# Hybrid encoder layer on one core: h of four blocks and two thirds of the adaLN modulation moved from the front phase into the projection phase

## What is computed

```python
ada = jax.nn.silu(c) @ p['w_ada'][l] + p['b_ada'][l]
sh1, sc1, gt1, sh2, sc2, gt2 = jnp.split(ada[:, None, :], 6, axis=-1)
h = rms_norm(x, p['norm_pre_mix'][l]) * (1 + sc1) + sh1
x = x + gt1 * rms_norm(token_mixer(h, p, l), p['norm_post_mix'][l])
h = rms_norm(x, p['norm_pre_ffn'][l]) * (1 + sc2) + sh2
y = expert_choice_ffn(h, p['w_router'][l], p['w_gate_e'][l], p['w_up_e'][l], p['w_down_e'][l])
return x + gt2 * rms_norm(y, p['norm_post_ffn'][l])
```

## Time and profile before

| | us |
|---|---|
| median of three runs | 3905.72 |
| range of the runs | 3895.16 to 3907.7 |
| the profiled execution | 3897.49 |
| its span | 3895.8 |
| front phase | 0 to 168.9 |
| projections and attention | 168.9 to about 972 |
| gated linear attention | about 972 to 1679 |
| mix | 1679 to about 2250 |
| route, experts, final | to 3895.8 |

### The profile page before, as it was taken

One profiled execution on the slowest core, in us unless ns is written; L12 is line 12 of the kernel. 1 busy time (PEld: TensorE's weight loads), 2 busy tenths in 40 slices (PEclk: granted clock), 3 DMA queues, 4 the chain that ended last, 5 costly groups with the idle time before them and its releaser, 6 DMA issues. The chain is left out here.

```text
span 3895.8 us, 56808 instructions
## 1 busy us (share of the span) xinstructions
PE 3536.0 (91%) x21432; PEld 2934.1 (75%) x21432; DVE 2169.3 (56%) x3920; ACT 1593.3 (41%) x2374; POOL 651.0 (17%) x709
## 2 busy tenths in 40 slices
PE   7699999998889999979999928999999999999991
PEld 3377777766667777757878728999999999999991
DVE  1344534554568888745545465565555555555555
ACT  1344545544334344334444303444444444443442
POOL 0010100101023443402322200011110001000005
PEclk9799999999999999989999858999999999999996
DMA  9733432421754554456555434555555555555567
GB/s 303 238 120 87 136 115 86 130 86 64 232 169 137 168 155 138 120 168 204 187 185 187 154 135 157 157 167 169 170 174 161 165 164 175 172 162 166 162 218 272
DMA packets 544843, 634.46 MB, mean 163 GB/s; under 512 B 77560, under 2 KB 431896, under 8 KB 543776
## 3 DMA queue, kind: packets, MB, share of 16 engines
q1 hardware_dynamic: 506960, 493.72, 40.4%
q0 software_dynamic: 35840, 123.75, 10.0%
q10 hardware_dynamic: 1872, 14.68, 0.9%
HBM read 505.20 MB, written 126.88 MB: 162 GB/s over the span
## 5 line engine op out<-in xcount | busy, mean ns | idle before, releaser
L2414 DVE TENSOR_TENSOR moe_w_lo<-moe_w_raw,moe_w_hi 128x2048 fp32r<-128x2048 f32 x192 | 439.9, 2291 | 371.5 <-ACT moe_w_hi L2362 338.5
L103 PE MATMUL moe_pg<-moe_x_hi,moe_w_hi 128*128 128x320 f32 x2048 | 635.5, 310 | 1.4 <-DVE moe_x_lo L2452 1.4
L104 PE MATMUL moe_pg<-moe_x_lo,moe_w_hi 128*128 128x320 f32 x2048 | 633.8, 309 | 0.0
L105 PE MATMUL moe_pg<-moe_x_hi,moe_w_lo 128*128 128x320 f32 x2048 | 633.8, 309 | 0.0
L2362 ACT CAST moe_w_hi<-moe_w_raw 128x2048 fp32r<-128x2048 f32 x192 | 364.9, 1900 | 158.2 <-DMA moe_w_raw<-in_w_gate_e_dram 81.2
L103 PEld LDWEIGHTS moe_pg<-moe_x_hi,moe_w_hi 128*128 128x128 f32 x2048 | 385.3, 188 | 2.4 <-issue 1.5
L104 PEld LDWEIGHTS moe_pg<-moe_x_lo,moe_w_hi 128*128 128x128 f32 x2048 | 385.4, 188 | 0.6
L105 PEld LDWEIGHTS moe_pg<-moe_x_hi,moe_w_lo 128*128 128x128 f32 x2048 | 385.3, 188 | 0.0
L103 PE MATMUL gla_pd<-gla_h_hi,gla_w_hi 128*128 128x512 f32 x640 | 261.1, 408 | 34.5 <-DVE gla_h_lo L1012 31.9
L103 PE MATMUL pa_pu<-pa_h_hi,pa_w_hi 128*128 128x512 f32 (+1 forms) x560 | 226.9, 405 | 37.4 <-DVE pa_h_lo L644 37.4
L105 PE MATMUL gla_pd<-gla_h_hi,gla_w_lo 128*128 128x512 f32 x640 | 252.4, 394 | 0.0
(11 more groups left out here) (326 smaller groups left out, 7664.0 us busy)
## 6 DMA issues: line engine op xcount, KB each, us to landing
moe_w_raw<-in_w_gate_e_dram SPq DMA_DIRECT2D x64, 1024.0 KB
moe_w_raw<-in_w_up_e_dram SPq DMA_DIRECT2D x64, 1024.0 KB
moe_w_raw<-in_w_down_e_dram SPq DMA_DIRECT2D x64, 1024.0 KB
gla_w_raw<-in_w_in_dram SPq DMA_DIRECT2D x80, 512.0 KB, 4.0
pa_w_raw<-in_w_in_dram SPq DMA_DIRECT2D x35, 1024.0 KB
front_w<-in_w_ada_dram SPq DMA_DIRECT2D x24, 1024.0 KB, 11.9
scratch_gate<-gla_sg POOLq DMA_DIRECT2D x80, 256.0 KB, 2.3
mix_sg<-scratch_gate SPq DMA_DIRECT2D x40, 512.0 KB, 4.6
```

What stands on the lines that cost most here:

```text
L103: pe.matmul(out, w_hi, x_hi, start=start, stop=False)
L104: pe.matmul(out, w_hi, x_lo, start=False, stop=False)
L105: return pe.matmul(out, w_lo, x_hi, start=False, stop=stop)
L2414: dve.tensor_tensor(w_lo[:, m % 2], w_raw[:, m % 2], w_hi[:, m % 2].bitcast(F32), ALU.subtract).then_inc(s_wlo, 1)
```

## The change

It edits three phases.

In the front, only the first eight chunks of `w_ada` and block 0 remain. All eight chunks have buffers of their own. cS is widened to 32 columns, the products of the eight k go to four groups of 32 PSUM partitions (two each), the four partial sums are added by a product with `pick`, which also turns them. The 2 MB of h are stored in two halves by SP. The gates and the second modulation are gone from here.

In the projections, each of the 16 tiles of blocks 1 to 4 is made in the block before: `load_x` on SP, `squares` on ACT, `rms` on POOL, `norm_x` on DVE, `turn_x` on TensorE (eight transposes into two of the three banks, behind units `TURNS`), `first_half` on ACT and `second_half` on DVE (behind units `EVICTS`), `store_h` on POOL. `load_h` moves from chunk 7 to chunk 9 and waits for the stores. In the last block, 16 units of `ada_rows` use the remaining 16 chunks of `w_ada`, loaded by POOL, and their rows go to scratch `ada`. Unit v is computed like k, and a new unit `vt` turns it with four transposes. The low-rank unit stacks the high and low half of its weights into 64 columns (16 products for 24), and `la` is one fp32r product of 96 rows that hold high, low and high halves.

In the mix phase, block 0 reads the rows of `ada` and makes `K.a2`, `K.b2`, `K.gate1` and `gate2` from them between its first units; the router bias moves by up to two chunks. `K.gate1` is now allocated behind the gated linear attention.

```diff
-    K.gate1 = K.sb("gate1", [P, 2, D])
+    K.cS = K.sb("cS", [P, KD, 2])
...
+                for n in range(NCH):
+                    sp.dma_start(w[:, n], wv[:, :, n * CW:(n + 1) * CW]).then_inc(s_w[n], 16)
+                    if n == 1:
+                        sp.dma_start(x[:], block_of(I, 0)).then_inc(s_x, 16)
+                for i in range(2):
+                    sp.wait_ge(s_ha, 2 * i + 2)
+                    sp.wait_ge(s_hd, 2 * i + 2)
+                    sp.dma_start(S["hT"][0][:, 4 * i * BLK:4 * (i + 1) * BLK],
+                                 hT[:, 4 * i:4 * i + 4].rearrange("p k n -> p (k n)")).then_inc(s_st, 16)
+                sp.wait_ge(s_st, 32)
...
+                    pe.wait_ge(s_w[n], 16)
                     for k in range(KD):
-                        mm = pe.matmul(pa[m % 2][0:2, n % 2 * CW:n % 2 * CW + CW], cS[:, k, :], w[:, n % RAW, k, :],
-                                       start=k == 0, stop=k == KD - 1)
+                        mm = pe.matmul(pa[n // 2][k % 4 * 32:k % 4 * 32 + 32, n % 2 * CW:n % 2 * CW + CW], cS[:, k, :],
+                                       w[:, n, k, :], start=k < 4, stop=k >= 4)
                     mm.then_inc(s_chunk, 1)
 
...
+                for n in range(NCH - 2):
+                    chunk(n)
                 pe.wait_ge(s_id, 4)
...
+BLOCK_UNITS = [("k", 0, 0), ("v", 0, 0), ("q", 0, 1), ("vt", 0, None), ("q", 1, 1), ("q", 2, 2), ("q", 3, 2), ("l", 0, 3),
...
+TURNS = {4: 0, 7: 1, 12: 2, 16: 3}
+SQUARES = {1: 0, 5: 1, 8: 2, 11: 3}
+NORMS = {2: 0, 6: 1, 10: 2, 14: 3}
+EVICTS = {5: 0, 8: 1, 13: 2, 17: 3}
+N_ADA = 16
+ADA = {j: n for n, j in enumerate([j for j, u in enumerate(BLOCK_UNITS) if u[0] not in ("la", "vt")][:N_ADA])}
+
...
+                    if b:
+                        for n in range(2):
+                            sp.wait_ge(s_hst[n], 32 * b)
...
+                    if b < NB - 1:
+                        load_x(4 * b)
+                        load_x(4 * b + 1)
...
+                        if c in (7, 8) and b < NB - 1:
+                            load_x(4 * b + c - 5)
+                        if c == 9 and b < NB - 1:
...
+                        wait(act, s_lat, b)
+                        act.copy(vT, bank[:]).then_inc(s_evac, 1)
+                    elif kind == "vt":
...
+                        act.copy(rank[0], bank[2 * RANK:4 * RANK, :]).then_inc(s_g, 1)
+                        act.wait_ge(s_gs, b + 1)
+                        act.copy(gl[0:2 * RANK, :], rank[1])
+                        act.copy(gl[4 * RANK:6 * RANK, :], rank[1]).then_inc(s_ghi, 1)
...
+                def squares(i):
+                    act.wait_ge(s_x[i % 2], 16 * (i // 2 + 1))
+                    wait(act, s_rstd, i)
+                    for n in range(2):
+                        wait(act, s_sq, 2 * i + n)
+                        act.activation(junk, x[:, i % 2, n * D // 2:(n + 1) * D // 2], ACT.Square,
+                                       accum_out=ss[:, n:n + 1]).then_inc(s_sq, 1)
+
+                def first_half(i):
+
+                    n = UNIT_NO["turn", i, 0]
+                    act.wait_ge(s_unit, n + 2)
+                    for k in range(KD // 2):
+                        ins = act.activation(x[:, i % 2, k * P:(k + 1) * P], pu[n % BANKS][:, k * P:(k + 1) * P], ACT.Identity,
+                                             bias=K.b1[:, 1, k:k + 1], scale=K.a1[:, 1, k:k + 1])
+                    ins.then_inc(s_ha, 1)
+
+                def read_ada(i):
+                    n = UNIT_NO["ada", i, 0]
+                    act.wait_ge(s_unit, n + 1)
+                    wait(act, s_rst[i % 2], 64 * (i // 2))
+                    act.copy(row[:, i % 2], pu[n % BANKS][:, 0:CW]).then_inc(s_row, 1)
+
                 split_w(0)
                 split_h(0)
...
+                        if b < NB - 1 and j in EVICTS:
+                            first_half(b * TPB + EVICTS[j])
+                        if b < NB - 1 and j in SQUARES:
+                            squares(b * TPB + SQUARES[j])
+                        if b == NB - 1 and j in ADA:
+                            read_ada(ADA[j])
...
+                def second_half(i):
+
+                    n = UNIT_NO["turn", i, 1]
+                    dve.wait_ge(s_unit, n + 1)
+                    for k in range(KD // 2, KD):
+                        ins = dve.tensor_scalar(x[:, i % 2, k * P:(k + 1) * P], pu[n % BANKS][:, (k - 4) * P:(k - 3) * P],
+                                                K.a1[:, 1, k:k + 1], K.b1[:, 1, k:k + 1], ALU.mult, ALU.add)
+                    ins.then_inc(s_hd, 1)
...
+                            dve.wait_ge(s_g, b + 1)
+                            dve.tensor_tensor(rank[1], pu[n % BANKS][0:2 * RANK, :], rank[0], ALU.add).then_inc(s_gs, 1)
+                            dve.wait_ge(s_ghi, b + 1)
+                            dve.tensor_tensor(gl[2 * RANK:4 * RANK, :], rank[1], gl[0:2 * RANK, :].bitcast(F32),
+                                              ALU.subtract).then_inc(s_glo, 1)
...
+                def store_h(i):
+                    pool.wait_ge(s_ha, i + 1)
+                    pool.wait_ge(s_hd, i + 1)
+                    b, t = i // TPB + 1, i % TPB
+                    pool.dma_start(S["hT"][b].rearrange("p (k n) -> p k n", n=BLK)[:, :, t * P:(t + 1) * P],
+                                   x[:, i % 2].rearrange("p (k n) -> p k n", n=P)).then_inc(s_hst[i % 2], 16)
+
+                ada = I["w_ada"][0].rearrange("(k p) n -> p k n", p=P)[:, :, 2 * D:6 * D]
+
+                def load_ada(i):
+                    if i >= N_ADA:
+                        return
+                    if i == 0:
+                        for n in range(2):
+                            pool.wait_ge(s_hst[n], 32 * (NB - 1))
+                    else:
+                        pool.wait_ge(s_unit, UNIT_NO["ada", i - 1, 0] + 1)
+                    for n in range(2):
+                        pool.dma_start(x[:, n].rearrange("p (k n) -> p k n", n=CW),
+                                       ada[:, 4 * n:4 * n + 4, i * CW:(i + 1) * CW]).then_inc(s_ada[n], 16)
+
...
+                    what, b, j = ORDER[n - BANKS]
+                    if what == "turn":
+                        pe.wait_ge(s_hd if j else s_ha, b + 1)
+                        return
+                    if what == "ada":
+                        pe.wait_ge(s_row, b + 1)
+                        return
...
+                def turn_x(i, half):
+                    n = UNIT_NO["turn", i, half]
+                    bank_free(n)
+                    pe.wait_ge(s_xn, i + 1)
+                    for k in range(4 * half, 4 * half + 4):
+                        ins = pe.transpose(pu[n % BANKS][:, k % 4 * P:(k % 4 + 1) * P], x[:, i % 2, k * P:(k + 1) * P], K.ident[:])
+                    ins.then_inc(s_unit, 1)
+
+                def ada_rows(i):
+
+                    n = UNIT_NO["ada", i, 0]
+                    bank_free(n)
+                    for k in range(KD):
+                        if k % 4 == 0:
+                            pe.wait_ge(s_ada[k // 4], 16 * (i + 1))
+                        ins = pe.matmul(pu[n % BANKS][k % 4 * 32:k % 4 * 32 + 2, 0:CW], K.cS[:, k, :],
+                                        x[:, k // 4, k % 4 * CW:(k % 4 + 1) * CW], start=k < 4, stop=k >= 4)
+                    ins.then_inc(s_unit, 1)
+
...
+                            rows = slice(0, 6 * RANK)
+                            mm = pe.matmul(bank[:], wa2[rows, i // 2, i % 2 * P:(i % 2 + 1) * P], gl[rows], start=True, stop=True)
+                        elif kind == "vt":
+                            pe.wait_ge(s_evac, evac_no(b, 1))
+                            for t in range(TPB):
+                                mm = pe.transpose(bank[:, t * P:(t + 1) * P], vT[:, t * P:(t + 1) * P], K.ident[:])
+                        elif kind == "l":
+                            s, m = c % 2, 2 * RANK
+                            for k in range(KD):
+                                if k == KD // 2 and (b, j) in MID:
+                                    step(MID[b, j])
+                                if k:
+                                    pe.matmul(bank[0:m, :], w_hi[:, s, k, 0:m], h_lo[:, k], start=False, stop=False)
+                                mm = pe.matmul(bank[0:2 * m, :], w_hi[:, s, k, 0:2 * m], h_hi[:, k], start=k == 0, stop=k == KD - 1)
+                                if k == 0:
+                                    pe.matmul(bank[0:m, :], w_hi[:, s, k, 0:m], h_lo[:, k], start=False, stop=False)
+                        elif kind == "gv":
...
+                        if b < NB - 1 and j in TURNS:
+                            turn_x(b * TPB + TURNS[j], 0)
+                            turn_x(b * TPB + TURNS[j], 1)
+                        if b == NB - 1 and j in ADA:
+                            ada_rows(ADA[j])
...
+                sp.dma_start(rows[0:8, :], S["ada"]).then_inc(s_rows, 16)
```

(72 more changed lines are left out.)

404 lines of the change are left out of this document (212 added, 192 removed).

## The result

The changed kernel takes 3924.98 us (median of 6 runs, 3921.72 to 3930.71), the kernel before 3901.72 beside it (median of 6, 3892.93 to 3907.86). The ratio is 1.0062, with a 95% interval of 1.0044 to 1.0080. The forecast was 3884: the range held the time, the sign was wrong.

The account below looks back on a forecast made before the run. The prediction took TensorE's work and waits to bound the projections, with half the front spent on `w_ada` chunks. Its terms, -120 - 23.5 - 13.4 - 4 + 17.3 + 83 + 15 + 16.8 + 4 + 12, gave -13: 3884 us, range 3842 to 3932.

Parts of the forecast that it names:

- the clock: Projections: eight of TensorE's new waits lower the granted clock, 1.8 us lost behind each, 15 us (bounds 0 to 25).
- The waits: Projections: TensorE waits for banks of turned tiles and the late fourth x tile, 83 us more (bounds 50 to 105).
- The front: Front phase: with eight chunks and one block left it ends at 49 us, 120 less (bounds 113 to 124).
- v turned: Projections: v computed like k plus four transposes and a drain saves 4.7 us in each of five blocks, 23.5.
- The low-rank unit: Projections: 16 products for 24 save 9 us at best; alternating 32 and 64 columns costs some, taken as -4 (-9 to +5).
- The log gate: Projections: one fp32r product saves 0.67 us, 20 times, 13.4; its ACT and DVE input chain is hidden by the gq unit.
- `ada_rows`: Last projection block: sixteen modulation units, column groups overlapping, 1.05 us each, 16.8 us more (upper bound 58).
- The rival with serial products: Last projection block: modulation products do not overlap across column groups, 41 us more, 3925 us in all; chance 0.15.
- Their loads: Last projection block: the first six modulation loads miss their window by up to 1 us, 4 in all (bounds 0 to 15).
- The mix phase: Mix phase: gate spreads 7.6, sixteen small products 1.4, small loads ahead of a weight 3: 12 us more (bounds 8 to 25).
- the forecast of 95: Projections as a whole: they grow by about 95 us, giving back what was left of the front's gain.
- The one with late transfers: x tiles and modulation chunks land 3 us later than priced, mix phase at upper bound: 45 us more, 3929; chance 0.25.

Follow-up runs that it names:

- Run 4: Changed kernel with TensorE given useless identity transposes in each of the five waits of a block, the waits left as they are: 3891.25 us, ratio 0.9963.
- run 1: Changed kernel with each turned tile read by ACT and DVE straight behind the step in which it was turned: 3845.51 us, ratio 0.9854.
- run 2: Changed kernel with ACT asking for the fourth x tile of a block (its squares) two units later: 3891.82 us, ratio 0.9968.
- run 3: Changed kernel with both early reading of the turned tiles and later squares of the fourth tile: 3812.36 us, ratio 0.9766.
- run 5: Changed kernel with the eight products of each modulation unit all in one column group: 3957.38 us, ratio 1.0143.
- run 6: Changed kernel with v, the low-rank unit and the log gates as they were before the change: 3992.70 us, ratio 1.0237.
- run 7: Kernel of run 8 with v alone as before the change, 96 products of 128 columns and no turning: 3841.70 us, ratio 0.9832.
- run 10: Kernel of run 8 with the mix phase's modulation rows loaded by ACT's queue at the phase start instead of SP's: 3799.78 us, ratio 0.9733.
- run 8: Kernel of run 3 with the last block's sixteen modulation units starting one projection unit later: 3805.66 us, ratio 0.9747.

## Why the prediction was wrong

**The step that failed is the clock.** The prediction wrote "Eight of the waits are longer than that gap: 15", at 1.8 us each. The price was near and the count was not, by the prediction's own list: a wait of 2.97 us was the one that had lowered the clock, and longer than that were 3.05 behind gq0, 5.3 and 3.4 at la2, and 6.65 behind gv1, four in each of four blocks: 16, not 8. 16 x 1.8 = 29. Run 4 measured 32. That the two agree so well is in part luck, for the trace counts otherwise. The two waits at la2 share one stretch at the lower clock; this is the one of block 1:

```profile
326.90:337.10 10.20, 5.21 (x11) 3.76 (x12) 2.72 (x8) 5.15 (x15) 2.40 (x5) 0.50 0.23 74
```

So the turned tiles have 14 such stretches: 4 behind gq0, 4 at la2, 4 behind gv1, and 2 of tile 0, in the blocks where its wait was 3.0 and 3.3. Three more lie at block boundaries, where the second gap is 1.9 to 2.0 us and was 1.4 to 1.6 in the kernel before, which has none in its blocks 1 to 4. One of these three is left in run 4: 32 us for the other 16 is 2.0 each. The first wait of the last block (5.8, for `w_ada`) costs some 3 more. With 29 in place of 15 the sum would have been +1; the terms below bring it near the measured +24.

**The waits** (83, bounds 50 to 105) were 88.6, each in its place, at its unit and near its size. Runs 1 to 3 show them causal: without them the projections lose 112, of which 77 is time in which TensorE stood (62.2 + 22.9, less the 8.8 that are left, is 76) and 35 is the same instructions done sooner.

**The front** (-120) came out at -117.7. The sixteen small products of `columns` took 5.0 us, not 1.4:

```profile
34.54 5.02 PE L227 MATMUL front_pc<-front_pick,front_row 128*128 128x2 f32 x32
```

The 1.4 was the price of another form: sixteen small turns of two rows each in the front of the kernel before (L262). The granted clock was 1.00 to 36.5 and 0.50 from 36.8 on, so at the upper clock they would still be some 3.6 (an estimate from these two stretches). The phase ended at 51.2 where 49 was reckoned.

**The units.** v turned (-23.5) gave the 4.7 a block that it was priced at, with v at full clock. The low-rank unit gave 9.35, not 4: the alternation between 32 and 64 columns costs nothing, 0.23 us from one product to the next, as between equal ones.

```profile
835.18 0.39 PE L988 MATMUL pa_pu<-pa_h_hi,pa_w_hi 128*64 128x512 f32 x1
835.41 0.39 PE L987 MATMUL pa_pu<-pa_h_lo,pa_w_hi 128*32 128x512 f32 x1
835.64 0.40 PE L988 MATMUL pa_pu<-pa_h_hi,pa_w_hi 128*64 128x512 f32 x1
```

The rule that the prediction weighed here (the Trainium skill, TensorEngine Tiling (Array Packing), Key Properties: a change of tiling mode drains TensorE) would have made the term +5; between these two widths the rows show no drain. The log gate (-13.4) saved 0.72 for 0.67 at full clock. Behind a wait the changed kernel's took 0.50 and 0.80 for 0.33. No wait for its chain on ACT and DVE appears.

**`ada_rows`** (16.8) took 0.97 a unit to the next one's first product, and 0.18 more lies between the step and it: 18.4 in all. The rival with serial products would have been 41 more; run 5, which has them serial, is 34.5 more. The Trainium skill (TensorE: Matmul & The Clock Gate, Part 3: Packing small matmuls) spoke against that rival with 2.38x for three groups; here it was 3.5x for four (3.62 to 1.04). **Their loads** (4) cost 8.9: 5.8 of it is the first, issued behind the block's last store. The window that the prediction compared was that of the later ones.

**The mix phase** (12, bounds 8 to 25) was 15.3: the wait 3.9 for 3, the column products 3.54 and 1.94 for 1.4 together, the spreads four times 1.98 to 2.8 for 7.6. These are 6 over their prices and the phase is 3.3 over its own, within what it differs by from one execution to the next.

**The account** for the projections, over the forecast of 95: clock 32 + 3 for 15, waits 5.6 more, `w_ada` 5 more, the block boundary 2.2 more (39.6 for 37.4), `ada_rows` 1.6 more, the low-rank unit 5 less: 29, where 31 was measured. Nothing large is unexplained. Two rivals came nearer to the measured time than the forecast and were wrong all the same. The one with serial modulation products gave 3925, the time measured, and run 5 refutes it. The one with late transfers gave 3929, but its x tiles landed as priced (6.2 us), and what it added at the fourth tile did not appear.

Not settled is why the clock falls behind the gaps of 1.5 and about 2 us at some block boundaries and not at others, nor behind which of the waits of about 2 us it falls.

## What to carry to other kernels

When transposes or other small work borrow banks of a rotating set, look at who gives the bank back and how many instructions stand ahead of that in its queue: here the same read, done one unit earlier, was worth 2% of the kernel. Price each new wait of TensorE twice, with its length and with the half-clock work behind it, and count those waits, and the stretches at half clock that they share, from the list of the waits. A cheap tile that is loaded late should be asked for at the last place that still suffices, not at the first.

## What the runs showed of the hardware

- A stream of 128-column products that starts at the lower clock can stay there: 96 of them took 20.2 us at 0.50 in blocks 0 and 2 of run 7, 10.6 at 1.00 in the others. In the changed kernel, units of 512-column products came back to 1.00 within themselves every time, after at most 13 of their 24 products (5.5 us). In the profiled execution of the kernel before, the unit v never stuck; with the waits that the change brings it did in 4 of 10 blocks (runs 6 and 7), and turning it took that away.
- Waits of TensorE of 1.9 to 2.2 us behind tile 2 lowered the clock in none of four places in run 3 and in run 10, in one in run 8 and in three in run 7: a wait of this length may cost clock or not. Without a longer wait ahead (tile 2 in run 2) 2.6 and twice 2.8 lowered it, 2.55 did not. In the changed kernel each of 3.0 us or more between two units did, at about 2 us a stretch. Behind the wait of 2.21 us in block 2 of run 7:

```profile
470.70:474.00 3.30, 3.30 (x9) 2.54 (x8) 0.47 (x1) 1.45 (x4) 1.80 (x4) 0.50 0.46 134
```

- 128 x 128 transposes issued in the waits kept the granted clock at 0.99 to 1.00 in all four blocks of run 4, where the changed kernel has 0.91 to 0.94.
- fp32r products of 32 and of 64 output columns in turn keep the pitch of equal ones, 0.23 us; fp32 products with two columns of weights in four column groups run four at a time (1.04 us for eight, 3.62 in one group).
